# One-hot rows built with one compare-and-multiply per token, and the gathered slots of the expert stage spread anew

## What is computed

```python
def peer_ffn(h, w_query, sub_keys, expert_u, expert_v):
    ...
    scores = jnp.einsum("thcd,hcnd->thcn", qry, sub_keys).astype(jnp.float32)
    s_top, i_top = lax.top_k(scores, P_TOPK)
    cand_s = (s_top[:, :, 0, :, None] + s_top[:, :, 1, None, :]).reshape(T, P_HEADS, P_TOPK * P_TOPK)
    cand_i = (i_top[:, :, 0, :, None] * N_KEYS + i_top[:, :, 1, None, :]).reshape(T, P_HEADS, P_TOPK * P_TOPK)
    best_s, best_pos = lax.top_k(cand_s, P_TOPK)
    expert_idx = jnp.take_along_axis(cand_i, best_pos, axis=-1)
    gates = jax.nn.softmax(best_s, axis=-1).astype(h.dtype)
    ...
        act = jax.nn.gelu(jnp.einsum("td,thkd->thk", hb, expert_u[eb]), approximate=False)
        return jnp.einsum("thk,thkd->td", act * gb, expert_v[eb])
```

## Time and profile before

| what | value |
|---|---|
| median of 3 runs | 2004.93 us (2002.63 to 2009.47) |
| the profiled execution, its own time | 2008.27 us |
| its span on the core | 2006.5 us |
| TensorE busy (matmul) | 1936.8 us, 97% |
| VectorE busy | 1503.3 us, 75% |
| ScalarE busy | 718.4 us, 36% |
| GpSimd busy | 459.2 us, 23% |

### The profile page before, as it was taken

The page is one execution under the profiler, slowest core; times in us unless marked ns, Lnnn a source line. Parts: engine busy times, 40 slices in busy tenths (PEclk is TensorE's granted clock), DMA queues, the critical chain, the costliest instruction groups (busy, mean ns, idle before and its releaser), DMA issues.

```text
span 2006.5 us, 27908 instructions
## 1 busy us (share of the span) xinstructions
PE 1936.8 (97%) x10341; PEld 1713.6 (85%) x10341; DVE 1503.3 (75%) x2742; ACT 718.4 (36%) x1327; POOL 459.2 (23%) x235
## 2 busy tenths in 40 slices
PE   5999999999999989999999999999999999999998
PEld 3889777789877878899999999999988888888886
DVE  5677645364476536787889999997689898889885
ACT  4110233010352243343443444444444444444443
POOL 0443210434102123101011511111222223223221
PEclk9999999999999999999999999999999999999999
DMA  6335410454212422257767688888999999999993
GB/s 254 105 105 177 138 63 21 142 173 147 63 43 84 147 85 85 84 171 257 231 227 259 214 325 299 296 303 301 413 384 401 402 400 400 401 401 402 397 368 120
DMA packets 212642, 465.92 MB, mean 232 GB/s; under 512 B 15624, under 2 KB 157120, under 8 KB 193344
## 3 DMA queue, kind: packets, MB, share of 16 engines
q1 hardware_dynamic: 194112, 330.47, 47.3%
q0 software_dynamic: 18432, 134.23, 16.9%
HBM read 410.12 MB, written 54.53 MB: 232 GB/s over the span
## 4 chain that ended last, share of the span: by engine, by line
PE 42%; DMA 8%; DVE 5%; ACT 1%; SPq 1%; issue 1%; POOLq 0%; POOL 0%; DVEq 0%; ACTq 0%
PE xin_ps_u L2075 22%; PE xin_out L2119 16%; DMA experts_hot<-act_scratch 6%; PE xin_out L2097 4%; DMA con_raw<-in_expert_u 2%; DVE over_v_vlo L2386 1%; SPq L2047 1%; DVE in_ulo L2237 1%; DVE experts_rows L1868 1%; DVE experts_acc L1887 1%; DVE xin_wt L2383 1%; ACT in_uhi L2148 0%; DVE xin_wlo L2388 0%; ACT L2190 0%; DVE over_s_stage L2251 0%
## 5 line engine op out<-in xcount | busy, mean ns | idle before, releaser
L1861 POOL DMA_INDIRECT experts_rows<-in_expert_rows,experts_idx x128 | 234.4, 1831 | 886.9 <-DVE experts_acc L1887 752.0
L2075 PE MATMUL xin_ps_u<-con_h_hi,in_uhi 128*128 128x384 f32 x1024 | 348.4, 340 | 10.3 <-DVE in_ulo L2237 8.1
L2075 PE MATMUL xin_ps_u<-con_h_lo,in_uhi 128*128 128x384 f32 x1024 | 342.9, 335 | 0.0
L2075 PE MATMUL xin_ps_u<-con_h_hi,in_ulo 128*128 128x384 f32 x1024 | 342.8, 335 | 0.0
L2119 PE MATMUL xin_out<-over_v_vhi,xin_whi 128*128 128x512 f32 x768 | 238.8, 389 | 2.5 <-DVE xin_wlo L2388 2.4
L2119 PE MATMUL xin_out<-over_v_vlo,xin_whi 128*128 128x512 f32 x768 | 238.4, 389 | 0.0
L2119 PE MATMUL xin_out<-over_v_vhi,xin_wlo 128*128 128x512 f32 x768 | 238.3, 389 | 0.0
L2237 DVE TENSOR_TENSOR in_ulo<-con_raw,in_uhi 128x1024 fp32r<-128x1024 f32 x127 | 155.4, 1223 | 79.0 <-ACT in_uhi L2148 75.2
L2075 PEld LDWEIGHTS xin_ps_u<-con_h_hi,in_uhi 128*128 128x128 f32 x1024 | 192.9, 188 | 14.5 <-DVE in_ulo L2237 11.9
L2075 PEld LDWEIGHTS xin_ps_u<-con_h_lo,in_uhi 128*128 128x128 f32 x1024 | 192.9, 188 | 0.0
L2075 PEld LDWEIGHTS xin_ps_u<-con_h_hi,in_ulo 128*128 128x128 f32 x1024 | 192.6, 188 | 0.0
(11 more groups left out here) (420 smaller groups left out, 3754.3 us busy)
## 6 DMA issues: line engine op xcount, KB each, us to landing
con_raw<-in_expert_u SPq DMA_DIRECT2D x128, 512.0 KB, 5.8
con_raw<-in_expert_v SPq DMA_DIRECT2D x128, 512.0 KB
con_raw<-in_w_in SPq DMA_DIRECT2D x36, 1024.0 KB, 5.8
act_scratch<-in_act SPq DMA_DIRECT2D x128, 192.0 KB
experts_hot<-act_scratch SPq DMA_DIRECT2D x128, 192.0 KB
gate_scratch<-in_stage SPq DMA_DIRECT2D x12, 1024.0 KB
gate_scratch<-over_s_stage SPq DMA_DIRECT2D x12, 1024.0 KB
experts_hot<-gate_scratch SPq DMA_DIRECT2D x16, 768.0 KB
```

The lines of the kernel that those rows point to most:

```text
L1861: pool.indirect_dma_start(out=self.rows[:, r % ROWS, :], out_offset=None, in_=table, in_offset=at).then_inc(self.row_in[r % ROWS], 16)
L2075: mm = pe.matmul(ps_u[s % 2][:, 0:TD], a[s % 2][:, k, :], m[:, k, P:T], start=(i == 0), stop=(i == 3 * KD - 1))
```

## The change

Two edits. In `gates`, the first compare over 8 tokens at once (into `hot_i`) and the multiplication of its result by the gates, two operations of 1024 elements each and a semaphore between them, are replaced by 8 operations of 128 elements: each compares the key numbers with one token's key and multiplies by that token's gate, both of them read as one value per partition. The compare into `hot_j` stays. In `slots_of_steps`, the rule for the slots of the first pass is another one in the gate steps and in the tail: a gate step now has a slot unless n % 4 is 1 (36 slots where there were 24), a tail step has one where n is even (10 where there were 15). The steps before are as they were (12 slots). So the first pass takes 58 slots in place of 51, and the second pass has 70 in place of 77.

```diff
--- before.py
+++ after.py
@@ -1905,7 +1905,7 @@
     inside = [[] for n in range(NEXP)]
     r = 0
     for n in range(N_SEARCH + R_STEPS + 4, NEXP):
-        if (n < N_ROUTE and n % 4 == 0) or N_ROUTE <= n < N_HOT0 or (N_HOT0 <= n < N_HOT0 + N_HOT and n % 2 == 0) or (n >= N_HOT0 + N_HOT and n % 4 != 3):
+        if (n < N_ROUTE and n % 4 == 0) or N_ROUTE <= n < N_HOT0 or (N_HOT0 <= n < N_HOT0 + N_HOT and n % 4 != 1) or (n >= N_HOT0 + N_HOT and n % 2 == 0):
             inside[n].append(r)
             r += 1
     outside = [[] for n in range(NEXP)]
@@ -2368,11 +2367,12 @@
                 wait(dve, g_done, 2 * (m - 1))
                 shape = [P, G_TOK, NK]
                 keys = con.iota[:].unsqueeze(1).to_broadcast(shape)
-                i_s, j_s, g_s = [slot[x][:, m * G_TOK:(m + 1) * G_TOK].unsqueeze(2).to_broadcast(shape) for x in range(3)]
-                dve.tensor_tensor(hot_i[m % 2], keys, i_s, ALU.is_equal).then_inc(is_row, 1)
+                j_s = slot[1][:, m * G_TOK:(m + 1) * G_TOK].unsqueeze(2).to_broadcast(shape)
                 dve.tensor_tensor(hot_j[m % 2], keys, j_s, ALU.is_equal)
-                dve.wait_ge(is_row, m + 1)
-                dve.tensor_tensor(hot_i[m % 2], hot_i[m % 2], g_s, ALU.mult).then_inc(hot_done, 1)
+                for t in range(G_TOK):
+                    i_t, g_t = [slot[x][:, m * G_TOK + t:m * G_TOK + t + 1] for x in (0, 2)]
+                    op = dve.tensor_scalar(hot_i[m % 2][:, t], con.iota[:], i_t, g_t, ALU.is_equal, ALU.mult)
+                op.then_inc(hot_done, 1)
 
             def weighted(n):
                 s = n % RING
```

More of the change, by code:

```diff
@@ L1964, in experts_block @@
         (u_done, gelu_done, chosen, exp_done, sub_done, pool_step, keys_done,
-         slots_t, slots_done, hot_done, g_done, staged, sum_inv, is_rank, is_row) = map(al.sem, (
+         slots_t, slots_done, hot_done, g_done, staged, sum_inv, is_rank) = map(al.sem, (
              "u_done", "gelu_done", "chosen", "exp_done", "sub_done",
-             "pool_step", "keys_done", "slots_t", "slots_done", "hot_done", "g_done", "staged", "sum_inv", "is_rank",
-             "is_row"))
+             "pool_step", "keys_done", "slots_t", "slots_done", "hot_done", "g_done", "staged", "sum_inv", "is_rank"))
         whi, wlo = [[al.sb(f"{n}{i}", [P, TD], F32R) for i in range(RING)] for n in ("whi", "wlo")]
```

## The result

The changed kernel takes 2014.48 us (median of 7 runs, 2012.84 to 2017.09), the kernel before 2004.93 us (7 runs). The ratio is 1.0041, with a 95% interval of 1.0028 to 1.0054: slower by 0.41%, 8 us (the two medians lie 9.6 us apart). The forecast was 2004.0 us and no change, in a range of 1998.0 to 2012.0. The profiled execution has a span of 2014.1 us against 2006.5, 7.6 us more.

| stretch | before, us | after, us | difference |
|---|---|---|---|
| up to block 0 of the first pass | 838.4 | 837.3 | -1.1 |
| blocks 0 to 59 | 259.2 | 259.3 | +0.1 |
| gate steps, 60 to 107 | 285.8 | 291.3 | +5.5 |
| blocks 108 to 111 | 20.9 | 27.8 | +6.9 |
| blocks 112 to 126 | 64.0 | 62.4 | -1.6 |

What follows compares the result with a forecast made beforehand. TensorE was taken to bound the gate steps, tail and second pass. Terms -0.4, 0, +1.0, -1.3 and -0.2 gave -0.9 us against the profiled 2008.27, 3.3 above the median: forecast 2004.0 us, range 1998.0 to 2012.0.

Steps and rivals of the forecast that it cites:

- What bounds the kernel: Gate steps: TensorE needs 5.95 us a step, VectorE 5.71, so TensorE is the bound by 0.24 us.
- I take 0.20: New one-hot operations in the gate steps: pace c of 0.20 us each, from a row with one per-partition value.
- my two bounds: Pace of the new one-hot operation: between 0.20 us (second value read beside the first) and 0.255 us (read after it).
- The formula: VectorE's mean gate step is 4.03 + 8c us: 5.63 at c = 0.20, its cover gone at c = 0.24.
- rival 1: Gate steps: the second per-partition value costs like the first, c = 0.255, +5.8 us, 2009.8 us; chance 0.17.
- Two long steps lose about 0.5 us, the short ones give it back: Gate steps: VectorE's uneven steps, about 6.2 and 5.0 us, even out through double-buffering; steady gain nil.
- +1.0 us: Tail, stall before block 110 (2.54 us): one added fetch delays the load, between nothing and 2.65 us, taken as +1.0.
- The gains: Tail's 1.32 us stall goes with 5 fewer gathers, -1.3 us; second pass's 0.41 us stall half counted, -0.2 us.
- Start of the gate steps, -0.4: TensorE's 0.4 us wait for a one-hot row goes, as the rows are done 0.67 us sooner each step.
- Rival 5: Gate steps: VectorE's small operations and POOL's fetches shut each other out, +45 us, 2050 us; chance 0.02.
- Rival 4: All stalls of the rows go, each a late DMA beside gathers: -6.2 us, 1998.8 us; chance 0.09.
- rival 3: Tail: whole 2.65 us before block 110, plus a new like-sized stall with slower clock; +5 us, 2010 us; chance 0.05.

Runs made afterwards that it cites:

- the first edit alone: The kernel before with the new one-hot rows in `gates` and the old slot rule: 2007.79 us, ratio 1.0011.
- the run with one value: The changed kernel with constant 1.0 in place of the per-partition gate, so each small operation reads one value: 2004.62 us, ratio 0.9998.
- the second edit alone: The kernel before with the new slot rule and the old one-hot rows in `gates`: 2021.85 us, ratio 1.0073.
- the quiet end: The changed kernel with slots moved: 30 at n = 60 to 103, none at 104 to 109, 9 later, 77 in the second pass: 2000.73 us, ratio 0.9961.

## Why the prediction was wrong

The outcome lies outside the range, on the slower side. By the prediction's own steps:

1. **What bounds the kernel**: right. TensorE set the gate steps, by 0.24 us; with the first edit alone nothing moved. (In the 40 slices of the kernel before, VectorE's digit is 9 in the gate steps only, then 7 and 6 in the tail and 8 or 9 in the second pass.)
2. **"I take 0.20" for the pace c: this step failed.** The measured pace is 0.256, the upper of my two bounds, 0.255: a second per-partition value costs 0.06 us like the first. The formula held: 4.03 + 8 x 0.256 = 6.08, measured 291.3 / 48 = 6.07 us. I had priced this as rival 1 with +5.8 and got +5.5, and gave it 0.17. The row chosen was the nearest, but a row with one value cannot tell what two cost; the only rows on it, a value costs 0.055 where there was none, spoke for adding it again.
3. **"Two long steps lose about 0.5 us, the short ones give it back"**: right for c = 0.20, as the run with one value shows.
4. **"+1.0 us" for the stall before block 110: the second step that failed.** It was 9.01 - 2.54 = +6.5 (the rest of the table's +6.9 is the slower clock behind it: the step of block 110 takes 6.10 us for 5.61). I took the 2.65 us of a gather's own transfer as the most that one can cost a load behind it. One added fetch came with 2.4 us where VectorE was on time, but taking it out of the changed kernel gave 3.5 us back. What I left out is that VectorE, once it is the bound, comes late to the tail: with the same slots the idle time is 4.93 us where it is on time (one value) and 9.01 where it is not. By the bytes, 1.26 MB more of gathers and 0.71 MB more of SP's queue moved in the changed kernel during the load than before, at 340 GB/s and not 368. Lateness alone does not give it: with the second edit alone VectorE is late too and both fetches are there, but 1.33 MB less was moved and the idle time is 5.20. Why SP's queue moves more ahead of the landing in one run than in another is open, and each run has one profile.
5. **The gains**: right in kind, and too small: 3.8 us where the sum had 1.3 + 0.2. The stall of 1.32 us and that of 0.41 us in the second pass are gone, with another 1.2 us at the last block of the first pass, which the sum did not have. The gain in the second pass is not owed to its 7 slots fewer: the quiet end has 77 slots there, as before, and no gap either.
6. **Start of the gate steps, -0.4**: right, with -0.3; the steps at n = 59 to 61 come to 5.89, 5.99 and 5.95 us after 5.89, 5.97 and 6.25.
7. **Rival 5, the shared ports**: VectorE was not held up. Timeline of POOL and of VectorE in the kernel after, where a fetch meets the small operations; then a fetch in the kernel before with VectorE idle, and one in the run with the second edit alone:

```profile
1255.03 1.68 POOL L1861 DMA_INDIRECT experts_rows<-in_expert_rows,experts_idx  x1 [4.98 <-DVE experts_acc L1887]
...
1255.82 2.12 DVE L2374 TENSOR_SCALAR experts_hot<-con_iota,in_slot 128x128 f32<-128x128 f32 x8
...
1381.99 0.94 POOL L1861 DMA_INDIRECT experts_rows<-in_expert_rows,experts_idx  x1 [10.22 <-DVE experts_acc L1887]
...
1386.87 6.23 POOL L1861 DMA_INDIRECT experts_rows<-in_expert_rows,experts_idx  x1 [5.20 <-DVE experts_acc L1887]
```

The fetch and the eight small operations overlap for 0.9 us, and the eight take 2.12 us as they do without a fetch. The fetch is the one that is longer: it takes 0.94 us where VectorE is idle and 1.68 us here, as beside VectorE's long operations. Beside the old one-hot rows it took up to 6.23 us, when VectorE ran five long operations without a pause (1386.53 to 1392.22 us). The maximum of 6223 ns in the earlier trace rows is of that kind, a meeting with the old operations; the prediction did not ask what made it. It cost the kernel nothing: VectorE waited 0.1 us for all its gathers. The Trainium skill, page "SBUF — State Buffer", section "Who interferes with whom", states that whichever of the two issues first has the shared ports for its whole instruction and the other is blocked. The long fetches would fit that; between a fetch and these small operations this trace doesn't show it. With constants in place of both values there is a sign of it: 8 of the 12 fetches that meet them take 2.07 us or more, and beside the other 4 one small operation starts 0.12 us late.

Rival 4's counter-argument, that the stall before block 110 hangs on SP's wait and not on gathers, was half right: with no gather in flight 1.36 of its 2.54 us stay.

The rivals were taken one at a time, each against the forecast's other terms. Rivals 1 and 3 are linked: where VectorE becomes the bound, it comes late to the next stage. Together they give 2004.93 + 5.8 + 4.95 = 2015.7 us, near the median of 2014.48, but part of that is luck: of rival 3's two stalls only one came, and it was larger than the two together. Luck of the same kind is in the run with one value: it has the pace that the forecast took and, at 2004.62 us, nearly its time, while its stall is 1.4 us dearer than the forecast's and its gains are over 2 us larger.

## What to carry to other kernels

Price an operation by a row with the same number of per-partition values; where none exists, add the cost once for each, and work out the case in which the busy engine passes the limit before spending what it saves. An engine that becomes the bound is late at the end of its stage too: look at which transfers it lets go there, and add up all the bytes that move while the next needed load is under way, not the largest single one. Background gathers belong where both the engine and the DMA engines have room, and away from the point where a burst of writes and a needed load go out together; there, they were worth more than the arithmetic saved: the same small operations gave 1.0041 with one placing of the slots and 0.9961 with another (0.9956 with the flush moved as well).

## What the runs showed of the hardware

- A VectorE operation on 128 x 128 f32 with two arithmetic steps starts every 0.135, 0.196 or 0.256 us with 0, 1 or 2 per-partition values. From the table of the Trainium skill, page "VectorE: DVE Perf Modes", section on the TRN2 errata, an estimate of 0.127 us follows at two elements a cycle; only the form with constants comes near.
- A 512 KB load behind a 1 MB flush took 6.21 us with no gather in flight, 7.40 and 7.64 with 0.84 and 0.85 MB of a gather moved meanwhile, and 9.79 to 13.87 with 1.05 to 2.36 MB. Both queues together moved 337 to 375 GB/s in the runs with gathers.
- The issue of a gather on POOL took 0.94 us with VectorE idle, 1.68 us beside most of its operations, and up to 6.23 us beside five of its operations of 1024 elements without a pause between them.
- With 77 gathered slots the second pass stays at TensorE's pace (1.1 us of gaps before, none in the quiet end), with 81 it has 4.2 us of gaps. The DMA share is 1.03 in both, at 395 and 397 GB/s; that is not the highest rate of this case, since the tail moved 408.
